# A transformer kernel whose expert layer gathers its tokens for two experts at once, from split rows

## The reference

```python
N_EXPERTS = 8; TOP_K = 2; D_FF_2 = 3584      # t: 256 tokens x 1024

def swiglu(t, w_gate, w_up, w_down):
    return (jax.nn.silu(t @ w_gate) * (t @ w_up)) @ w_down

def moe_swiglu(h, router_w, w_gate, w_up, w_down):
    t = h.reshape(bsz * seq, d)
    logits = (t @ router_w).astype(jnp.float32)
    top_v, top_i = lax.top_k(logits, TOP_K)
    top_p = jax.nn.softmax(top_v, axis=-1)
    gates = jnp.sum(jax.nn.one_hot(top_i, N_EXPERTS) * top_p[..., None], axis=1)
    out = jnp.zeros_like(t)
    for e in range(N_EXPERTS):
        out = out + gates[:, e:e + 1] * swiglu(t, w_gate[e], w_up[e], w_down[e])
    return out
```

## Time and profile before

| | us |
|---|---|
| median of 3 runs | 2780.44 |
| lowest, highest | 2779.2, 2781.05 |
| the profiled execution | 2776.66 |
| its span in the trace | 2774.7 |
| TensorE busy | 2699.8 (97%) |
| VectorE busy | 2100.5 (76%) |
| ScalarE busy | 1683.4 (61%) |

### The profile page before, as it was taken

One profiled execution on the slowest core, in us unless ns is written; L12 is line 12 of the kernel. 1 busy time (PEld: TensorE's weight loads), 2 busy tenths in 40 slices (PEclk: granted clock), 3 DMA queues, 4 the chain that ended last, 5 costly groups with the idle time before them and its releaser, 6 DMA issues.

```text
span 2774.7 us, 42780 instructions
## 1 busy us (share of the span) xinstructions
PE 2699.8 (97%) x18396; PEld 2484.2 (90%) x18396; DVE 2100.5 (76%) x2094; ACT 1683.4 (61%) x1824; POOL 71.7 (3%) x114
## 2 busy tenths in 40 slices
PE   7999999999999999999999999999999999999998
PEld 7999999999999999989899999888888888888886
DVE  5777758877677568867677766788898989888896
ACT  4555447654555456554577644676677767777675
POOL 1000000001000000000011000000000000000000
PEclk9999999999999999999999999999999999999999
DMA  7645548746445477543788633798998989898894
GB/s 243 178 139 168 163 155 276 272 133 181 149 133 183 147 242 258 198 127 107 243 299 296 212 92 110 277 380 338 351 363 341 371 339 379 336 377 345 334 375 181
DMA packets 304403, 679.22 MB, mean 245 GB/s; under 512 B 16560, under 2 KB 238032, under 8 KB 261072
## 3 DMA queue, kind: packets, MB, share of 16 engines
q1 hardware_dynamic: 288832, 617.67, 62.1%
q0 software_dynamic: 15376, 58.75, 6.5%
HBM read 675.32 MB, written 4.69 MB: 245 GB/s over the span
## 4 chain that ended last, share of the span: by engine, by line
PE 77%; DVE 11%; ACT 8%; issue 2%; DMA 1%; POOL 0%; SPq 0%; ACTq 0%; DVEq 0%
PE bank L562 73%; DVE ew_lo L1978 4%; ACT ring_tail L2184 3%; ACT w_hi L2096 2%; DVE ring_low L1459 1%; PE bank L1223 1%; PE bank L664 1%; PE bank L642 1%; DVE ring_low L1339 1%; PE bank L602 1%; DVE ring_tail L1416 0%; PE bank L706 0%; DVE xT L1723 0%; ACT ew_hi L2475 0%; DMA ring_head<-in_w_mix_out 0%
## 5 line engine op out<-in xcount | busy, mean ns | idle before, releaser
L1978 DVE TENSOR_TENSOR ew_lo<-ring_head,ew_hi 128x2048 fp32r<-128x2048 f32 x336 | 759.1, 2286 | 41.6 <-ACT ew_hi L2475 41.6
L2475 ACT CAST ew_hi<-ring_head 128x2048 fp32r<-128x2048 f32 x336 | 640.4, 1915 | 224.0 <-PE bank L562 223.9
L562 PE MATMUL bank<-xs_hi,ring_low 128*128 128x256 f32 (+1 forms) x2608 | 512.4, 283 | 0.0
L562 PEld LDWEIGHTS bank<-xs_hi,ring_low 128*128 128x128 f32 (+1 forms) x2608 | 415.2, 190 | 1.8 <-issue 0.7
L562 PE MATMUL bank<-ew_hi,xe_hi 128*128 128x512 f32 x896 | 353.3, 394 | 0.0
L562 PE MATMUL bank<-ew_hi,xe_lo 128*128 128x512 f32 x896 | 349.2, 390 | 0.0
L562 PE MATMUL bank<-ew_lo,xe_hi 128*128 128x512 f32 x896 | 348.6, 389 | 0.0
L562 PE MATMUL bank<-x_hi,w_hi 128*128 128x256 f32 x1152 | 320.7, 285 | 8.6 <-DVE ring_low L1459 5.7
L562 PE MATMUL bank<-x_hi,ring_low 128*128 128x256 f32 x1152 | 316.5, 281 | 0.0
L1459 DVE TENSOR_TENSOR ring_low<-ring_head,w_hi 128x2048 fp32r<-128x2048 f32 x105 | 239.8, 2289 | 100.8 <-ACT w_hi L2096 100.8
L562 PE MATMUL bank<-x_lo,w_hi 128*128 128x256 f32 x1080 | 296.8, 281 | 0.0
(11 more groups left out here) (444 smaller groups left out, 5440.2 us busy)
## 6 DMA issues: line engine op xcount, KB each, us to landing
ring_head<-in_moe_w_gate SPq DMA_DIRECT2D x112, 1024.0 KB, 7.2
ring_head<-in_moe_w_up SPq DMA_DIRECT2D x112, 1024.0 KB, 6.9
ring_head<-in_moe_w_down SPq DMA_DIRECT2D x112, 1024.0 KB, 7.1
ring_head<-in_w_in SPq DMA_DIRECT2D x82, 1024.0 KB, 5.4
ring_tail<-in_ada_w POOLq DMA_DIRECT2D x48, 1024.0 KB, 10.3
ring_head<-in_ffn_w_in SPq DMA_DIRECT2D x44, 1024.0 KB, 7.1
ring_head<-in_ffn_w_out SPq DMA_DIRECT2D x22, 1024.0 KB, 9.0
ring_head<-in_xa_kv SPq DMA_DIRECT2D x16, 1024.0 KB, 5.4
```

The source lines that it names most:

```text
L562: ins = nc.tensor.matmul(out, lhsT, rhs, start=start, stop=stop, **kw)
L1978: v.tensor_tensor(ew_lo[:, h, :], ring(c % 6), ew_hi[:, h, :].bitcast(F32), ALU.subtract).then_inc(w_used[c % 6], 1)
L2475: a.copy(ew_hi[:, (e * len(PARTS) + c) % DEPTH_HI, :], ring(c % 6)).then_inc(f.count(part_hi), 1)
```

## The change

The gather is made once for two experts, ahead of experts 0, 2, 4 and 6 and not ahead of the odd ones. `select` gets 256 columns, 128 for each of the two, and is written as fp32r. The rows of the tokens are kept split: `rows_hi`, cast to fp32r by the four ScalarE copies that filled `htok`, and `rows_lo`, four VectorE subtractions more before the first expert. The gather multiplies high rows and low rows by `select` apart, in the form for fp32r operands, with 256 columns moving: 8 groups of 4 matmuls through banks 2, 3 and 7 (`gather_order`). What comes out of a high group is already the high part and is copied by ScalarE, what comes out of a low group is the low part and is copied (not subtracted) by VectorE, a quarter of the tiles at a time. From the fourth group on the gather waits for the copy that frees its bank. The transposes of `weigh` move ahead of the gather. `xe_hi` and `xe_lo` make way for `gathered_hi` and `gathered_lo`, laid over `gates`, of which each expert uses its half of the columns.

```diff
--- before.py
+++ after.py
@@ -157,6 +157,8 @@
             ring_low = in_scope(twin, "ring_low", 6, CH, dt=F32R)
         ring_head = sb("ring_head", 6, CH)
         xT = sb("xT", KD, TOK)
+        with ExitStack() as twin:
+            _, rows_hi = (in_scope(twin, n, 2, D, dt=F32R) for n in ("under_rows", "rows_hi"))
         work = sb("work", 2 * CH)
         yT = tiles(work[:, 0:CH], KD)
         merged = tiles(work[:, CH:2 * CH], KD)
@@ -165,8 +167,11 @@
             ye_lo, ye_hi = (in_scope(twin, n, D, dt=F32R) for n in ("ye_lo", "ye_hi"))
         memT = sb("memT", KD, TOK)
         with ExitStack() as twin:
-            _, back = (in_scope(twin, n, k * TOK, dt=F32R) for n, k in (("under_back", 2), ("back", 1)))
+            select = in_scope(twin, "select", 2, TOK, dt=F32R)
+            back = in_scope(twin, "back", TOK, dt=F32R)
         kb = sb("kb", 4, TOK)
+        with ExitStack() as twin:
+            _, gathered_hi, gathered_lo = (in_scope(twin, n, KD, TOK, dt=F32R) for n in ("under_gathered", "gathered_hi", "gathered_lo"))
         gates = sb("gates", 24, TOK)
         flat = gates[:, :, :].rearrange("p n t -> p (n t)")
         squares = tiles(flat[:, 0:CH], KD)
@@ -224,7 +229,7 @@
                 x_hi, x_lo = (in_scope(ffns, n, KD, TOK, dt=F32R) for n in ("x_hi", "x_lo"))
                 act_hi, act_lo = (in_scope(ffns, n, 2, 2, TOK, dt=F32R) for n in ("act_hi", "act_lo"))
         ew_hi, ew_lo = (sb(n, DEPTH_HI, CH, dt=F32R) for n in ("ew_hi", "ew_lo"))
-        xe_hi, xe_lo = (sb(n, KD, P, dt=F32R) for n in ("xe_hi", "xe_lo"))
+        rows_lo = sb("rows_lo", 2, D, dt=F32R)
         eact_hi, eact_lo = (sb(n, ETILES, P, dt=F32R) for n in ("eact_hi", "eact_lo"))
 
         highs = [chunk_high[:, :], ring_low[:, 5, :], ring_low[:, 2, :]]
@@ -281,9 +286,9 @@
 
             return bank[out_of[k // 2]][:, (k % 2) * TOK:(k % 2 + 1) * TOK]
 
-        htok = work[:, CH:2 * CH].rearrange("p (t d) -> p t d", t=2)
         share = small[:, 57:58]
-        select, weigh = (tiles(kb[:, i, :], 2) for i in range(2))
+        weigh = tiles(kb[:, 3, :], 2)
+        gather_order = [(0, 0, 2), (1, 0, 3), (0, 1, 7), (1, 1, 2), (0, 2, 3), (1, 2, 7), (0, 3, 2), (1, 3, 3)]
         esilu, eact = flat[:, 0:EC], flat[:, 1024:1024 + EC]
         both = tiles(bank[6], ETILES)
         slots = const[:, C_IOTA:C_IOTA + P]
@@ -1186,18 +1191,23 @@
 
                     def gather():
 
-
-                        for q in range(2):
-                            for i in range(4):
+                        his, los = f.now(gather_hi), f.now(gather_free)
+                        for n, (low, q, b) in enumerate(gather_order):
+                            if n in (3, 5, 7):
+                                pe.wait_ge(gather_hi, his + (n - 1) // 2)
+                            elif n in (4, 6):
+                                pe.wait_ge(gather_free, los + (n - 2) // 2)
+                            for i in range(2):
                                 for t in range(2):
-                                    k = 4 * q + i
-                                    mm(bank[2 + q][:, i * P:(i + 1) * P], htok[:, t, k * P:(k + 1) * P], select[:, t, :],
-                                       t == 0, t == 1, gather_full if (i, t) == (3, 1) else None)
+                                    k = 2 * q + i
+                                    mm(bank[b][:, i * TOK:(i + 1) * TOK], (rows_hi, rows_lo)[low][:, t, k * P:(k + 1) * P], select[:, t, :],
+                                       t == 0, t == 1, gather_full if (i, t) == (1, 1) else None)
 
                     def shares(e):
 
                         for t in range(2):
-                            mm(bank[1][:, 0:1], select[:, t, :], picks[:, e, 2 + t:3 + t], t == 0, t == 1, share_full if t else None)
+                            chosen_by = select[:, t, (e % 2) * P:(e % 2 + 1) * P].bitcast(F32)
+                            mm(bank[1][:, 0:1], chosen_by, picks[:, e, 2 + t:3 + t], t == 0, t == 1, share_full if t else None)
 
                     def part(e, c, k):
 
@@ -1210,10 +1220,12 @@
                             hi, lo = part(e, FIRST[kind, step] + i, WK)
                             for k in range(WK):
                                 t = WK * i + k
-                                if fresh and t % 4 == 0:
+                                if fresh and t % 2 == 0:
+                                    pe.wait_ge(gather_hi, f.next(gather_hi))
                                     pe.wait_ge(gather_free, f.next(gather_free))
-                                for x, w, last in ((xe_hi, hi, False), (xe_hi, lo, False), (xe_lo, hi, True)):
-                                    mm(bank[b][:, :], x[:, t, :], w[:, k, :], t == 0 and w is hi and x is xe_hi, t == KD - 1 and last,
+                                mine = slice((e % 2) * P, (e % 2 + 1) * P)
+                                for x, w, last in ((gathered_hi, hi, False), (gathered_hi, lo, False), (gathered_lo, hi, True)):
+                                    mm(bank[b][:, :], x[:, t, mine], w[:, k, :], t == 0 and w is hi and x is gathered_hi, t == KD - 1 and last,
                                        part_done if last and k == WK - 1 else None)
 
                     def turn():
@@ -1262,7 +1274,7 @@
                         for e in range(EXPERTS):
                             if e:
                                 pe.wait_ge(back_free, f.next(back_free))
-                            widen(e, "gate", 0, 0, True)
+                            widen(e, "gate", 0, 0, e % 2 == 0)
                             widen(e, "up", 0, 2)
                             if e:
                                 result()
@@ -1281,13 +1293,11 @@
                             pe.wait_ge(gate_silu, f.next(gate_silu))
                             turn()
                             pe.wait_ge(select_ready, f.next(select_ready))
-                            if e < EXPERTS - 1:
-
-                                gather()
-
                             for t in range(2):
                                 ins = nc.tensor.transpose(bank[0][:, t * P:(t + 1) * P], weigh[:, t, :], ident)
                             ins.then_inc(f.count(back_full), 1)
+                            if e % 2 and e < EXPERTS - 1:
+                                gather()
                             if e < EXPERTS - 1:
                                 shares(e + 1)
                             down(e, STEPS - 1)
@@ -1964,6 +1974,12 @@
                     dve.wait_ge(f.last, f.now(f.last))
                     v.tensor_tensor(picks[:, 0:EXPERTS, 2:4].rearrange("p e t -> p t e"), route[:, :, :], second[:, :, :], ALU.add).then_inc(f.count(vector_step), 1)
 
+                    for q in range(4):
+                        part = slice(512 * (q % 2), 512 * (q % 2) + 512)
+                        f.bump(bank_full[4 + q])
+                        dve.wait_ge(src_hi, 14 * DEPTH + q + 1)
+                        v.tensor_tensor(rows_lo[:, q // 2, part], bank[4 + q], rows_hi[:, q // 2, part].bitcast(F32),
+                                        ALU.subtract).then_inc(f.count(bank_free[4 + q]), 1)
                     dve.wait_ge(bank_full[0], f.next(bank_full[0]))
                     v.tensor_tensor(picks[:, 0:EXPERTS, 0:2].rearrange("p e t -> p t e"), tiles(bank[0][:, 0:16], 2), chosen[:, :, :],
                                     ALU.mult).then_inc(f.count(vector_step), 1)
@@ -1989,17 +2005,24 @@
                         v.tensor_tensor(eact_lo[:, :, :], both, eact_hi[:, :, :].bitcast(F32), ALU.subtract).then_inc(f.count(eact_ready), 1)
 
                     def gathered(q):
-                        dve.wait_ge(gather_hi, f.next(gather_hi))
-                        ks = slice(4 * q, 4 * q + 4)
-                        v.tensor_tensor(xe_lo[:, ks, :], tiles(bank[2 + q][:, :], 4), xe_hi[:, ks, :].bitcast(F32),
-                                        ALU.subtract).then_inc(f.count(gather_free), 1)
+                        dve.wait_ge(gather_full, f.next(gather_full, 2))
+                        v.tensor_copy(gathered_lo[:, 2 * q:2 * q + 2, :], pairs((3, 2, 7, 3)[q])).then_inc(f.count(gather_free), 1)
+
+                    def chosen_pair(e):
+
+                        for t in range(2):
+                            for a in range(2):
+                                v.tensor_scalar(select[:, t, a * P:(a + 1) * P], slots, picks[:, e + a, t:t + 1], None,
+                                                ALU.is_equal).then_inc(f.count(select_ready if t and a else vector_step), 1)
 
                     def selections(e):
 
+                        more = e % 2 and e < EXPERTS - 1
                         for t in range(2):
-                            v.tensor_scalar(weigh[:, t, :], slots, picks[:, e, t:t + 1], None, ALU.is_equal).then_inc(f.count(vector_step), 1)
-                        for t in range(2):
```

(33 more changed lines are left out.)

## The result

The changed kernel took 2791.91 us (2785.78 to 2794.32) where the kernel before took 2779.2 (2775.86 to 2781.05): 1.0041 of it, 95% interval 1.0028 to 1.0053: **slower, by 0.4%**. A second, longer series gave 2786.55 against 2780.96: 1.0027, 1.0018 to 1.0036. The forecast was 2766.7, 0.995.

A forecast was written before the change was run, and what follows sets the result against it. TensorE's stream through the eight experts was taken as the bound, with the ScalarE-to-VectorE chain close by at passages. Terms -16.1 - 0.2 + 2.6 = -13.7 us gave 2766.7 us from 2780.44; range 2763.0 to 2772.5.

The forecast's parts named there:

- something slower or neutral that I don't see: Whole kernel: an unforeseen slower or neutral outcome, no size given; chance 0.03.
- The even passage: From an even to an odd expert, four times: no gather, next turn() 4.03 us earlier each, 16.1 in all.
- Rival (a): Even-to-odd passages: ScalarE and VectorE stay last, each gains 3.2 us and not 4.03, time 2770; chance 0.14.
- The gather: Gather for two experts: 32 matmuls at 0.12 us, 3.84 us in place of 7.14.
- the ties: Odd-to-even gather: waits for bank-freeing copies nearly met, 0 to 0.2 us each, 0.2 in sum.
- The three passages: From an odd to an even expert, three times: 28.4 us in place of 28.43, gaining 0.2 in all.
- Rival (e): Gather matmuls run at full-precision rate, 14.3 us a gather, time about 2807; chance 0.02.
- The start: Ahead of the first expert, once: late start, longer gather and two stalls lose 2.6 us.
- (b): First gather: the clock falls, costing 2 to 5 us, time 2769 to 2772; chance 0.12.
- (c): Every pair gather: the clock falls; at 10 us each, 20 us lost, time 2787; chance 0.03.
- Rival (d): Expert weights: DMA becomes the bound, a pair takes 246.0 us, time 2773.5; chance 0.04.

The follow-up runs named there:

- 224-byte kernel: The changed kernel with gathered_hi and gathered_lo placed 224 bytes earlier: 2770.23 us against 2780.32 for the kernel before, 0.9964.
- the fastest kernel: The 224-byte kernel with weight copy and subtraction moved behind the start's gathered copies, last turns of even experts and expert 7 in halves: 2766.55 us, 0.9946 of before.
- e4: The changed kernel with rows_lo and gathered_hi exchanging places, so gathered_hi lies at 212384 and gathered_lo stays: 2781.75 us.

## Why the prediction was wrong, point by point

**The term that was not in the sum.** Forecast for the layer and its start: -13.7 us. With the tiles at the weights' phase it came out at -10.4, and their place added 17.7, together +7.3. The step that failed is the sentence "The only thing different is the passage from one expert to the next": I priced all widening matmuls at the 0.227 of the rows of `xe_*`, in the passages and, as no change at all, in the steps between them, and never asked whether the new operand is the old one in all that the rows could depend on. They took 0.233, and 14.5 of the 17.7 us lie outside the passages. The diff said plainly that it lies elsewhere; no row of before shows another place, so there was nothing to price it by, but an unknown of 2688 matmuls deserved a bound. The widths of my range were made of terms of 0.2 to 3 us; this one is 6 ns, 2688 times. The outcome fell in the 0.03 that I had left for something slower or neutral that I don't see.

**The even passage: -12.1, not -16.1.** The step that failed is the path "TensorE: T0 + 0.23 + 0.36 + 23.72": transposes, shares, and then at once the last `down`, at T0+0.59. The gather stood between the `turn()` and the `down`, 3.57 us long, and under it ScalarE and VectorE made `eact_hi` and `eact_lo`. I had read that VectorE was done with it at T0+1.51, used the row for what VectorE does next, and not for who waits for it. With the gather gone, so is the cover:

```profile
1890.93 0.60 PE L1235 MATMUL bank<-const,gates 128*128 128x128 f32 x4
1891.37 0.38 PE L1297 MATMUL bank<-const,kb 128*128 128x128 f32 x2
1891.59 0.51 PE L567 MATMUL bank<-picks,select 128*128 128x1 f32 x4
1892.93 0.73 PE L567 MATMUL bank<-ew_hi,eact_hi 128*128 128x512 f32 x2 [0.84 <-DVE eact_lo L2005]
```

T0 is 1891.37 here, and `down` starts at T0+1.56, 0.97 late. Its first two matmuls then take 0.73 and not the 0.62 of later pairs; they do so in before too (0.72), and my 24 x 0.227 left that 0.1 out. With both, T0+25.4 is what the 224-byte kernel has (25.83 between starts of turns, less 0.44), against 24.4 forecast; the slow matmuls make it 25.87 in after. The waits of the whole layer name it: five times up to 1.2 us, four even passages and the end of expert 7, the one passage of before that had no gather:

```profile
PE bank L567 <- DVE eact_lo L2005: 4.5, 5, 1.2
```

That end stands in the profile of before too, in the timeline of TensorE at expert 7:

```profile
2747.79 0.60 PE L1223 MATMUL bank<-const,gates 128*128 128x128 f32 x4
2748.23 0.38 PE L1289 MATMUL bank<-const,kb 128*128 128x128 f32 x2
2749.79 0.73 PE L562 MATMUL bank<-ew_hi,eact_hi 128*128 128x512 f32 x2 [1.18 <-DVE eact_lo L1989]
```

The case without a gather was there to be read. I had put VectorE's chain (24.4) and TensorE's own (24.31) in a tie. The tie did not come about, as TensorE got a full us later; the wait for `xT` is gone, as I said it would be, in after as in the 224-byte kernel, but for a reason that I did not give. Rival (a) had the right size for the passage (3.2 gained; 3.0 measured) and the wrong mechanism.

**The gather: right.** 32 matmuls with 256 moving columns, in after at the passage 1 to 2:

```profile
2014.84 0.71 PE L567 MATMUL bank<-select,rows_hi 128*128 128x256 f32 x4
2015.39 0.63 PE L567 MATMUL bank<-select,rows_lo 128*128 128x256 f32 x4
...
2017.92 0.64 PE L567 MATMUL bank<-select,rows_hi 128*128 128x256 f32 x4
2018.40 0.63 PE L567 MATMUL bank<-select,rows_lo 128*128 128x256 f32 x4
2018.87 0.50 PE L567 MATMUL bank<-picks,select 128*128 128x1 f32 x4
2019.23 0.71 PE L567 MATMUL bank<-ew_hi,eact_hi 128*128 128x512 f32 x2
```

From 2014.84 to the shares at 2018.87 are 4.03 us; 3.84 and 0.2 of stalls were forecast. But for the first two, the starts within a group are 0.115 to 0.122 apart, and the fourth, fifth and seventh group come 0.08, 0.09 and 0.01 late: the ties, of the size that I gave them. The three passages, at the good place, gained 0.22 in all, and 0.2 was forecast. Rival (e), full-precision rate, is out. T0 (2014.70) to the last `down` is 4.53, forecast 4.63. The passage is 28.35 in the 224-byte kernel (28.4 forecast), 28.8 in after, 0.1 outside what I gave, and that is again the place.

**The start: right.** +2.41 where I had 2.6, and by the two stalls I named: group 5 behind VectorE's weight subtraction and group 8 behind ScalarE's weight copy. Counted by starts against an even pace of 0.475 a group they are 0.80 and 0.33 (0.9 and 0.4 forecast); the idle time in the rows, 0.63 and 0.16, is less, as the matmuls before run on into it. The gather began 0.85 later behind the router than before (0.94 forecast), with TensorE idle for 0.95 until `select` was there.

```profile
1771.39 0.74 PE L567 MATMUL bank<-select,rows_hi 128*128 128x256 f32 x4 [0.95 <-DVE select L2015]
...
1774.19 0.74 PE L567 MATMUL bank<-select,rows_hi 128*128 128x256 f32 x4 [0.63 <-DVE gathered_lo L2009]
...
1776.05 0.74 PE L567 MATMUL bank<-select,rows_lo 128*128 128x256 f32 x4 [0.16 <-ACT gathered_hi L2519]
```

**Rivals (b) and (c), the clock: no.** In after it was granted in full through the first gather with its stalls (4.82 us of work in 5.70, first row), through the second (second row), and through the layer (the window of 980 us above):

```profile
1771.30:1777.00 5.70, 4.82 (x37) 4.40 (x37) 5.70 (x6) 3.98 (x5) 0.00 (x0) 1.00 0.34 131
...
2014.80:2019.20 4.40, 4.40 (x39) 4.35 (x37) 2.80 (x5) 3.11 (x6) 0.00 (x0) 1.00 0.83 302
```

The Trainium skill, TensorE: Matmul & The Clock Gate, "A second HAM failure mode: psum-queue depth-cycling", would have made (c) the outcome; no fall is in these rows, neither where the groups came 0.08 and 0.09 late nor where the first gather paused for 0.80 and 0.33, so this case does not bear it out. Longer or more frequent pauses were not tried. The outcome was slower, as (c) had it, but by none of its mechanism.

**Rival (d), the DMA: no.** ScalarE never waits for a transfer in the layer, not in the fastest kernel either, where two experts (88.1 MB) take 2 x (5 x 16.79 + 11.35) + 25.35 + 28.75 = 244.7 us, 360 GB/s, less than the 246.0 that the rival gave them.

**What stays open.** Why 32 bytes against the moving tile cost 6 ns and not more or less, and why the kernel with the same place in 64 but not in 512 (one kernel, 192 bytes off) has 229 and not 227; other distances that are multiples of 64, 128 and 256 among them, were not tried, nor any that is not a multiple of 32. That the stretch up to the router varied by up to 10 us between profiles with the time at 1.2 GHz is seen, its trigger not.

## What to carry to other kernels

When a change gives an operand of the innermost matmul a new home, its address is part of the change: multiply any possible few ns by the number of matmuls before you sum the rest, and put the tile at the same distance from a multiple of 64 bytes (better, of 512) as the one that streams against it. When you take work off the path that sets the end, list what ran under it and who waits for that; look for a place in the same profile where the work is already absent, as the last expert here.

## What the runs showed of the hardware

The spacing of back-to-back 128x512 single-pass matmuls, each with a new stationary tile and at the full clock, depends on where the stationary tile starts against the moving one: 227 ns with both at the same distance from a multiple of 512 bytes, 229 with the same from a multiple of 64 only (one kernel), 233 where they are 32 apart in 64 (five kernels, at two distances in 512). A tile out of place costs in the distance from the matmul before and in the distance to the next (e4). The spacing does not depend on the tile's own address (227 at 212384, at 110496, and with weights and tiles moved by 32 together) nor on the stride from tile to tile (233 at 512 as at 1024 bytes). The Trainium skill, TensorE: Matmul & The Clock Gate, "Step-by-step: what each phase is for", says that the two operands are read by ports of their own and that loading the next stationary tile takes nothing from the running matmul; from that I would have expected 32 bytes between them to change nothing. The kernel before with 32 bytes put in disagrees, by 20.8 us over 4032 matmuls. That it is the reading of the two tiles that meets is likely, but no run here shows it.
